# Two 256-column products in place of one of 512, and one 256-column sum, in a float32 two-block transformer kernel

## The chip, the cores and the metric

The kernel runs on one core of a Trainium2 chip. The metric is the device time of one execution in microseconds (us), the median of three runs. The page of the profile comes from one further, profiled execution.

## The reference

256 tokens of width 2048 pass through two transformer blocks, all in float32. The first has 16 heads of causal attention with forget gates and a feed-forward part with a short convolution. The second has 4 heads of gated linear attention, 8 heads of dilated attention and a gated feed-forward part. The matrices are what costs time:

```python
# block 1
q, k, v, f_logit = jnp.split(h @ w_in, [hd, 2 * hd, 3 * hd], axis=-1)      # 2048 x (3 * 2048 + 16)
...
h = h + attention(...) @ w_out                                              # 2048 x 2048
up = rms_norm(h) @ w_up                                                     # 2048 x 2 * 5632
h = h + (jax.nn.silu(gate) * val) @ w_down                                  # 5632 x 2048
# block 2
x = x + mix @ w_out[l]
h2 = rms_norm_2(x, norm2_g[l])
x = x + (jax.nn.silu(h2 @ w_gate[l]) * (h2 @ w_up[l])) @ w_down[l]
```

## The kernel before, in words

Activations stand transposed: 128 features on the partitions, 256 tokens (S) along the free axis. Every large matrix is cut into blocks of 128 x 128, and eight blocks make a unit of 512 KB. There are 784 units, and they pass through a ring of four slots. For each unit SyncE starts one transfer into `raw`; ScalarE copies it into `whi` (line 729), rounded to the format in which TensorE multiplies at its full rate; VectorE subtracts (line 1053) and gets `wlo`, what the rounding dropped. Activations are split in the same way: `xs`, `mix` and `hid2` hold for each 128 features 256 columns of the high part and, right behind, 256 of the low part (`x[:, kc, 0, :]` and `x[:, kc, 1, :]`).

A product in nearly full float32 precision is then the sum of three: high weights by high x, high weights by low x, low weights by high x. TensorE does this in `unit` (lines 370 to 382): for the eight blocks one product each of `whi` with all 512 columns of x (line 378), then for the eight blocks one product each of `wlo` with the 256 high columns (line 381), added to the right half of the bank. An output chunk of 128 features so ends as two halves of a PSUM bank of 512 float32 columns, and VectorE adds them in `fold` (line 1059), a reduction over pairs into `folded_t`. The instruction behind it reads `folded_t`: the residual sum (line 1067), the scaling by the norm (`take`, line 1093) or line 1219 for one tile of the linear attention.

The order of the work is written out by hand, one queue for each engine, tied by semaphores. `lo_ready` counts split units and lets TensorE begin a unit; `unit_used` counts finished ones and lets ScalarE refill the slot; `chunk_out` counts chunks that VectorE has taken out of a bank and lets TensorE use it again. The ring runs three units ahead (`AHEAD`). Between units TensorE has small products of the attention heads (lines 412 to 526). Four banks `acc` take the large sums, four more the small ones. The units 0 to 95 are the projections ahead of block 1's heads, then come 32 of the output projection, 176 of up, 88 of down, and the same again for block 2. The first eight blocks are in `first_half` (lines 614 to 623), where high and low products take turns as x arrives.

`chunk_folded` is a second counter: `fold` and `narrow_copy` raise it, and `narrow_sum` on TensorE (line 410) waits for it.

Of the kernel before, what the change touches and what calls it, by code (L numbers as in the profile page):

```python
# [30 lines left out]
ALU = mybir.AluOpType  # L31
ACT = mybir.ActivationFunctionType
AX_X = mybir.AxisListType.X

P = 128
S = 256
# [62 lines left out]
def build(nc, wstream, narrow_w, xt, vectors, identity, dist_onehot, rel_bias, gate_w2, scan_keep, gla_mask, fox_mask, out):  # L99
    with ExitStack() as ctx:  # L100
# [8 lines left out]
        whi = [sb(f"whi{i}", [P, UW], F32R) for i in range(RING)]  # L109
# [259 lines left out]
        def _(pe):  # L369
            def unit(pos, k, blocks, x):  # L370

                slot = pos.slot(k)
                pe.wait_ge(lo_ready, pos.unit(k) + 1)
                for j, (bank_no, kc, first, last, late) in enumerate(blocks):
                    if late:
                        pe.wait_ge(*late)
                    w_hi = whi[slot][:, j * P:(j + 1) * P]
                    pe.matmul(acc[bank_no][:, :], w_hi, x[:, kc, :, :].rearrange("p a s -> p (a s)"), start=first, stop=False)  # L378
                for j, (bank_no, kc, first, last, late) in enumerate(blocks):
                    w_lo = wlo[slot][:, j * P:(j + 1) * P]  # L380
                    mm = pe.matmul(acc[bank_no][:, S:2 * S], w_lo, x[:, kc, 0, :], start=False, stop=last)  # L381
                mm.then_inc(unit_used, 1)

            def half(pos, k, bank_no, part, x, late=None):
# [22 lines left out]
                    if kc >= KC - 4:  # L407
                        mm.then_inc(narrow_done, 1)

            def narrow_sum(chunk):  # L410
                pe.wait_ge(chunk_folded, chunk + 1)
                pe.matmul(b_turn[0:16, 0:S], quarter_sum[:, 0:16], folded_t[:, :], start=True, stop=True).then_inc(narrow_summed, 1)

            def norm_mean(n):
# [199 lines left out]
            def first_half():  # L614
                pe.wait_ge(first_lo, 1)
                for kc in range(BLOCKS):
                    if kc == BLOCKS // 2:
                        pe.wait_ge(lo_ready, 1)
                    pe.wait_ge(xs_ready, kc + 1)
                    cols = slice(kc * P, (kc + 1) * P)  # L620
                    pe.matmul(acc[1][:, :], whi[0][:, cols], xs[:, kc, :, :].rearrange("p a s -> p (a s)"), start=kc == 0, stop=False)
                    mm = pe.matmul(acc[1][:, S:2 * S], wlo[0][:, cols], xs[:, kc, 0, :], start=False, stop=False)
                mm.then_inc(unit_used, 1)

            first = Pos(L0.unit_heads)
# [43 lines left out]
            for c in range(6):  # L669
                pe.wait_ge(chunk_out, L1.chunk_in if c == 1 or c == 2 else L1.chunk_heads + c - 2)  # L670
                for part in range(2):
                    k = 2 * c + part
                    late = {}
                    if c == 0:
                        late = {8 * part: (xs_ready, 2 * KC + 8 * (part + 1) - 1), 8 * part + 7: (xs_ready, 2 * KC + 8 * (part + 1))}
                    half(Pos(L1.unit_heads), k, 1 + c % 3, part, xs, late)
                    if k == 1:
                        norm_mean(2)
                        narrow(1)
                    if k == 2:  # L680
                        narrow_sum(L1.chunk_in)
                    if k == 3:
                        gates()
                    if k == 7:
                        gla_intra(0)
                    if k == 9:
                        gla_turn_v(0, False)
                    if k == 10:
                        gla_chunk_states(0)
# [358 lines left out]
        def _(dve):  # L1048
# [3 lines left out]
                dve.wait_ge(hi_ready, pos.unit(k) + 1)  # L1052
                dve.tensor_tensor(wlo[slot][:, :], raw[slot][:, :], whi[slot][:, :], ALU.subtract).then_inc(lo_ready, 1)  # L1053

            def fold(rows, bank_no, chunk):

                if not isinstance(chunk, int) or chunk:
                    dve.wait_ge(chunk_out, chunk)
                dve.tensor_reduce(folded_t[0:rows, :], acc[bank_no][0:rows, :].rearrange("p (a s) -> p s a", a=2),  # L1059
                                  AX_X, ALU.add).then_inc(chunk_folded, 1)  # L1060
                dve.wait_ge(chunk_folded, chunk + 1)

            def add_residual(pos, k, c, chunk, bank_no):

                dve.wait_ge(unit_used, pos.unit(k))
                fold(P, bank_no, chunk)
                dve.tensor_tensor(xres[:, c, :], folded_t[:, :], xres[:, c, :], ALU.add).then_inc(chunk_out, 1)

            def norm_chunk(n, c, par, chunk_no):
                norm_lo(n, c, chunk_no)  # L1070
# [17 lines left out]
            def take(dst, bank_no, last_unit, chunk):  # L1088

                dve.wait_ge(unit_used, last_unit + 1)  # L1090
                rows = dst.shape[0]
                fold(rows, bank_no, chunk)
                dve.tensor_tensor(dst, folded_t[0:rows, :], rstd[0:rows, :], ALU.mult).then_inc(chunk_out, 1)  # L1093


            def square_low(n, which):
# [97 lines left out]
            def gla_step(g, s, pos, lag, own=True):  # L1194
# [20 lines left out]
                    return  # L1215
                if s == (2 if lag else 3):
                    dve.wait_ge(unit_used, chunk(0) + 1)
                    fold(P, 1, L1.chunk_heads + 6 * g)
                    dve.scalar_tensor_tensor(out=g_q[:, :], in0=folded_t[:, :], scalar=float(P) ** -0.5, in1=rstd[:, :],
                                             op0=ALU.mult, op1=ALU.mult).then_inc(chunk_out, 1)  # L1220
                if s == 4:
                    take(g_k[:, :], 2, chunk(1), L1.chunk_heads + 6 * g + 1)
# [425 lines left out]
```

## Time and profile before

| | |
|---|---|
| median of 3 runs | 2276.18 us (2275.83 to 2277.05) |
| profiled execution, its time | 2276.7 us |
| its span | 2274.8 us |
| PE busy | 2260.0 us (99%), 13190 products |
| weight loads (PEld) busy | 1980.8 us (87%), 13190 |
| VectorE (DVE) busy | 1623.9 us (71%) |
| ScalarE (ACT) busy | 1230.4 us (54%) |
| transfers | 421.82 MB, mean 185 GB/s |

"Busy" is the union of the records of an engine. A product's record goes from its start to the end of its passage through the array, so records of products in a row overlap, and the mean length of a record is not the distance between two. Weight loads have a row of their own, since they run beside the product in front. The chain of waits is followed back from the last instruction; its pieces don't overlap, so the length of a piece of eight products is eight times the distance between them. Its times at a start differ a little from those of the timeline, since a piece begins where the one before ended.

### The profile page before, as it was taken

The numbers are of one execution on the slowest core, as the hardware profiler recorded it, in microseconds if no ns is written. First come the engines' busy times: TensorE is split into PE (matmuls) and PEld (weight loads), VectorE is DVE, ScalarE is ACT, GpSimd is POOL, SyncE is SP. The second block draws the span as 40 slices with busy tenths as digits, with TensorE's granted clock in tenths as the row PEclk, the third lists the DMA queues.
The fourth block names the chain that finished last, engine by engine and source line by source line (L and its number), as shares of the span: only waits on it lengthen the run. The fifth ranks groups of instructions, "written<-read, shape, count | busy, mean of one in ns | idle before, by whom it ended". The sixth has DMA issues, their size and how long they took to land.

```text
span 2274.8 us, 39123 instructions
## 1 busy us (share of the span) xinstructions
PE 2260.0 (99%) x13190; PEld 1980.8 (87%) x13190; DVE 1623.9 (71%) x2378; ACT 1230.4 (54%) x1614; POOL 53.1 (2%) x78
## 2 busy tenths in 40 slices
PE   8999999999999999999999999999999999999999
PEld 6888888888888888888888888888888888888888
DVE  7877777888888888555567577777666676664554
ACT  6777765655555555444465577655444444443332
POOL 1111100000000000000000000000000000000000
PEclk9999999999999999999999999999999999999999
DMA  6555555555555555655545555555555555555654
GB/s 203 193 176 183 183 169 191 187 193 191 189 192 185 193 189 186 198 194 187 192 154 187 161 168 166 168 192 190 190 193 188 190 192 188 191 191 199 203 198 134
DMA packets 118593, 421.82 MB, mean 185 GB/s; under 512 B 13773, under 2 KB 15973, under 8 KB 118544
## 3 DMA queue, kind: packets, MB, share of 16 engines
q1 hardware_dynamic: 113760, 413.19, 55.2%
q0 software_dynamic: 2048, 5.39, 0.9%
q10 hardware_dynamic: 2736, 2.58, 0.3%
q8 instruction: 31, 0.51, 0.1%
q14 instruction: 18, 0.15, 0.0%
HBM read 418.98 MB, written 3.70 MB: 186 GB/s over the span
## 4 chain that ended last, share of the span: by engine, by line
PE 98%; DVE 1%; ACT 0%; DMA 0%; issue 0%; SPq 0%; DVEq 0%
PE acc L378 63%; PE acc L381 32%; PE b_score L435 0%; PE b_turn L440 0%; DMA xres<-xt 0%; PE b_mean L425 0%; PE b_mean L446 0%; PE b_mean L426 0%; PE b_val L432 0%; PE b_mean L447 0%; PE b_score L434 0%; PE b_mean L448 0%; ACT xs L857 0%; PE b_mean L518 0%; PE b_mean L515 0%; PE b_score L502 0%
## 5 line engine op out<-in xcount | busy, mean ns | idle before, releaser
L729 ACT ACTIVATE whi<-raw 128x1024 fp32r<-128x1024 f32 x783 | 826.3, 1059 | 826.0 <-PE acc L381 815.1
L1053 DVE TENSOR_TENSOR wlo<-raw,whi 128x1024 fp32r<-128x1024 f32 x783 | 959.9, 1229 | 376.3 <-ACT whi L729 374.3
L378 PE MATMUL acc<-xs,whi 128*128 128x512 f32 x4344 | 1094.9, 395 | 2.2 <-DVE wlo L1053 1.8
L378 PEld LDWEIGHTS acc<-xs,whi 128*128 128x128 f32 x4344 | 781.9, 188 | 146.5 <-issue 5.1
L381 PEld LDWEIGHTS acc<-xs,wlo 128*128 128x128 f32 x4344 | 583.4, 188 | 44.3
L381 PE MATMUL acc<-xs,wlo 128*128 128x256 f32 x4344 | 593.9, 279 | 0.0
L378 PE MATMUL acc<-hid,whi 128*128 128x512 f32 x1408 | 351.0, 392 | 0.0
L1059 DVE TENSOR_REDUCE folded_t<-acc 128x256 f32<-128x512 f32 x336 | 231.9, 690 | 137.9 <-PE acc L381 128.2
L378 PEld LDWEIGHTS acc<-hid,whi 128*128 128x128 f32 x1408 | 251.9, 188 | 43.2
L381 PEld LDWEIGHTS acc<-hid,wlo 128*128 128x128 f32 x1408 | 188.3, 188 | 14.4
L381 PE MATMUL acc<-hid,wlo 128*128 128x256 f32 x1408 | 191.6, 278 | 0.0
L378 PE MATMUL acc<-mix,whi 128*128 128x512 f32 x512 | 128.6, 394 | 0.0
L378 PEld LDWEIGHTS acc<-mix,whi 128*128 128x128 f32 x512 | 91.9, 188 | 16.5 <-DVE mix L1151 0.5
L381 PEld LDWEIGHTS acc<-mix,wlo 128*128 128x128 f32 x512 | 68.5, 188 | 5.2
L381 PE MATMUL acc<-mix,wlo 128*128 128x256 f32 x512 | 69.8, 279 | 0.0
L845 ACT ACTIVATE hid<-hid 128x256 f32 (+1 forms) x88 | 36.1, 410 | 53.5 <-DVE hid L1277 53.3
L1119 DVE SCALAR_TENSOR_TENSOR qk_n<-qk,qk_gain,rstd_qk 128x256 f32<-128x256 f32 x48 | 21.4, 488 | 44.2 <-ACT rstd_qk L756 44.2
L1093 DVE TENSOR_TENSOR up_g<-folded_t,rstd 128x256 f32<-128x256 f32 x88 | 37.5, 426 | 3.0
L1093 DVE TENSOR_TENSOR up_v<-folded_t,rstd 128x256 f32<-128x256 f32 x88 | 37.5, 426 | 3.0
L1281 DVE TENSOR_TENSOR hid<-hid,hid 128x256 f32 (+1 forms) x88 | 36.9, 419 | 1.0 <-ACT hid L845 1.0
L830 ACT ACTIVATE tap_g<-up_g,vec 128x256 f32<-128x256 f32 x44 | 26.5, 602 | 16.2 <-DVE up_g L1093 16.2
L838 ACT ACTIVATE tap_v<-up_v,vec 128x256 f32<-128x256 f32 x44 | 26.5, 602 | 15.1 <-DVE up_v L1093 15.0
(190 smaller groups left out, 1001.6 us busy)
## 6 DMA issues: line engine op xcount, KB each, us to landing
raw<-wstream SPq DMA_DIRECT2D x783, 512.0 KB, 4.0
decay_row<-decay_scratch POOLq DMA_DIRECT2D x16, 128.0 KB, 3.7
out<-xres ACTq DMA_DIRECT2D x16, 128.0 KB, 2.4
xres<-xt SPq DMA_DIRECT2D x3, 512.0 KB, 8.4
dist_scratch<-bias_scratch POOLq DMA_DIRECT2D x8, 192.0 KB, 4.6
toeplitz<-dist_scratch POOLq DMA_DIRECT2D x8, 128.0 KB, 3.9
xres<-xt SPq DMA_DIRECT2D x2, 256.0 KB, 4.6
raw<-wstream SPq DMA_DIRECT2D x2, 256.0 KB, 5.6
```

The lines of the kernel that those rows point to most:

```text
L378: pe.matmul(acc[bank_no][:, :], w_hi, x[:, kc, :, :].rearrange("p a s -> p (a s)"), start=first, stop=False)
L381: mm = pe.matmul(acc[bank_no][:, S:2 * S], w_lo, x[:, kc, 0, :], start=False, stop=last)
L729: act.activation(whi[slot][:, :], raw[slot][:, :], ACT.Copy).then_inc(hi_ready, 1)
L830: act.activation(tap_g[:, :], up_g[:, 0:S], ACT.Identity, scale=column("conv0", j), bias=column("convb", j)).then_inc(tap0, 1)
L838: act.activation(tap_v[:, :], up_v[:, 0:S], ACT.Identity, scale=column("conv0", FC + j), bias=column("convb", FC + j)).then_inc(tap0, 1)
L845: act.activation(hid2[:, j, 0, :], hid[:, :], ACT.Copy).then_inc(hid_hi_ready, 1)
L1053: dve.tensor_tensor(wlo[slot][:, :], raw[slot][:, :], whi[slot][:, :], ALU.subtract).then_inc(lo_ready, 1)
L1059: dve.tensor_reduce(folded_t[0:rows, :], acc[bank_no][0:rows, :].rearrange("p (a s) -> p s a", a=2), AX_X, ALU.add).then_inc(chunk_folded, 1)
L1093: dve.tensor_tensor(dst, folded_t[0:rows, :], rstd[0:rows, :], ALU.mult).then_inc(chunk_out, 1)
L1119: dve.scalar_tensor_tensor(out=qk_n[:, a, :], in0=qk[:, a, :], scalar=qk_gain[:, col + a:col + a + 1], in1=rstd_qk[:, a, :], op0=ALU.mult, ...
L1281: dve.tensor_tensor(hid2[:, j, 1, :], hid[:, :], hid2[:, j, 0, :], ALU.subtract).then_inc(hid_split, 1)
```

## The change

In `unit` the product with 512 columns becomes two runs: eight products of `whi` with the 256 high columns, then eight of `whi` with the 256 low columns, then, as before, eight of `wlo` with the high columns. All three add to columns 0 to 255 of the bank. `first_half` does the same for each of its blocks, without the runs. `fold` is gone: VectorE's instruction that used to read `folded_t` reads the bank. `chunk_folded` is raised by `narrow_copy` alone, so `narrow_sum` waits for 1 and 2.

```diff
--- before.py
+++ after.py
@@ -375,10 +375,13 @@
                     if late:
                         pe.wait_ge(*late)
                     w_hi = whi[slot][:, j * P:(j + 1) * P]
-                    pe.matmul(acc[bank_no][:, :], w_hi, x[:, kc, :, :].rearrange("p a s -> p (a s)"), start=first, stop=False)
+                    pe.matmul(acc[bank_no][:, 0:S], w_hi, x[:, kc, 0, :], start=first, stop=False)
+                for j, (bank_no, kc, first, last, late) in enumerate(blocks):
+                    w_hi = whi[slot][:, j * P:(j + 1) * P]
+                    pe.matmul(acc[bank_no][:, 0:S], w_hi, x[:, kc, 1, :], start=False, stop=False)
                 for j, (bank_no, kc, first, last, late) in enumerate(blocks):
                     w_lo = wlo[slot][:, j * P:(j + 1) * P]
-                    mm = pe.matmul(acc[bank_no][:, S:2 * S], w_lo, x[:, kc, 0, :], start=False, stop=last)
+                    mm = pe.matmul(acc[bank_no][:, 0:S], w_lo, x[:, kc, 0, :], start=False, stop=last)
                 mm.then_inc(unit_used, 1)
 
             def half(pos, k, bank_no, part, x, late=None):
@@ -407,8 +410,8 @@
                     if kc >= KC - 4:
                         mm.then_inc(narrow_done, 1)
 
-            def narrow_sum(chunk):
-                pe.wait_ge(chunk_folded, chunk + 1)
+            def narrow_sum(n):
+                pe.wait_ge(chunk_folded, n + 1)
                 pe.matmul(b_turn[0:16, 0:S], quarter_sum[:, 0:16], folded_t[:, :], start=True, stop=True).then_inc(narrow_summed, 1)
 
             def norm_mean(n):
@@ -618,8 +621,9 @@
                         pe.wait_ge(lo_ready, 1)
                     pe.wait_ge(xs_ready, kc + 1)
                     cols = slice(kc * P, (kc + 1) * P)
-                    pe.matmul(acc[1][:, :], whi[0][:, cols], xs[:, kc, :, :].rearrange("p a s -> p (a s)"), start=kc == 0, stop=False)
-                    mm = pe.matmul(acc[1][:, S:2 * S], wlo[0][:, cols], xs[:, kc, 0, :], start=False, stop=False)
+                    pe.matmul(acc[1][:, 0:S], whi[0][:, cols], xs[:, kc, 0, :], start=kc == 0, stop=False)
+                    pe.matmul(acc[1][:, 0:S], whi[0][:, cols], xs[:, kc, 1, :], start=False, stop=False)
+                    mm = pe.matmul(acc[1][:, 0:S], wlo[0][:, cols], xs[:, kc, 0, :], start=False, stop=False)
                 mm.then_inc(unit_used, 1)
 
             first = Pos(L0.unit_heads)
@@ -678,7 +682,7 @@
                         norm_mean(2)
                         narrow(1)
                     if k == 2:
-                        narrow_sum(L1.chunk_in)
+                        narrow_sum(1)
                     if k == 3:
                         gates()
                     if k == 7:
@@ -1052,19 +1056,10 @@
                 dve.wait_ge(hi_ready, pos.unit(k) + 1)
                 dve.tensor_tensor(wlo[slot][:, :], raw[slot][:, :], whi[slot][:, :], ALU.subtract).then_inc(lo_ready, 1)
 
-            def fold(rows, bank_no, chunk):
-
-                if not isinstance(chunk, int) or chunk:
-                    dve.wait_ge(chunk_out, chunk)
-                dve.tensor_reduce(folded_t[0:rows, :], acc[bank_no][0:rows, :].rearrange("p (a s) -> p s a", a=2),
-                                  AX_X, ALU.add).then_inc(chunk_folded, 1)
-                dve.wait_ge(chunk_folded, chunk + 1)
-
             def add_residual(pos, k, c, chunk, bank_no):
 
                 dve.wait_ge(unit_used, pos.unit(k))
-                fold(P, bank_no, chunk)
-                dve.tensor_tensor(xres[:, c, :], folded_t[:, :], xres[:, c, :], ALU.add).then_inc(chunk_out, 1)
+                dve.tensor_tensor(xres[:, c, :], acc[bank_no][:, 0:S], xres[:, c, :], ALU.add).then_inc(chunk_out, 1)
 
             def norm_chunk(n, c, par, chunk_no):
                 norm_lo(n, c, chunk_no)
@@ -1089,8 +1084,7 @@
 
                 dve.wait_ge(unit_used, last_unit + 1)
                 rows = dst.shape[0]
-                fold(rows, bank_no, chunk)
-                dve.tensor_tensor(dst, folded_t[0:rows, :], rstd[0:rows, :], ALU.mult).then_inc(chunk_out, 1)
+                dve.tensor_tensor(dst, acc[bank_no][0:rows, 0:S], rstd[0:rows, :], ALU.mult).then_inc(chunk_out, 1)
 
 
             def square_low(n, which):
@@ -1215,8 +1209,7 @@
                     return
                 if s == (2 if lag else 3):
                     dve.wait_ge(unit_used, chunk(0) + 1)
-                    fold(P, 1, L1.chunk_heads + 6 * g)
-                    dve.scalar_tensor_tensor(out=g_q[:, :], in0=folded_t[:, :], scalar=float(P) ** -0.5, in1=rstd[:, :],
+                    dve.scalar_tensor_tensor(out=g_q[:, :], in0=acc[1][:, 0:S], scalar=float(P) ** -0.5, in1=rstd[:, :],
                                              op0=ALU.mult, op1=ALU.mult).then_inc(chunk_out, 1)
                 if s == 4:
                     take(g_k[:, :], 2, chunk(1), L1.chunk_heads + 6 * g + 1)
```

TensorE's queue in the loop over the attention heads of block 1, in the kernel before (`xs` is the split x; x8 are eight products in a row; REGISTER_ALU and ISA rows are waits and registers):

```order
L373 ISA
L378 MATMUL acc<-xs,whi 128x512 x8
L381 MATMUL acc<-xs,wlo 128x256 x8
L373 REGISTER_ALU
L378 MATMUL acc<-xs,whi 128x512 x8
L381 MATMUL acc<-xs,wlo 128x256 x8
L444 REGISTER_ALU
L446 MATMUL b_mean<-probs_t,v_tok 128x128
L447 MATMUL b_mean<-probs_t,v_tok 128x128
L448 MATMUL b_mean<-probs_t,v_tok 128x128
```

and in the changed kernel (lines 449 to 451 are the former 446 to 448):

```order
L373 REGISTER_ALU
L378 MATMUL acc<-xs,whi 128x256 x8
L381 MATMUL acc<-xs,whi 128x256 x8
L384 MATMUL acc<-xs,wlo 128x256 x8
L373 REGISTER_ALU
L378 MATMUL acc<-xs,whi 128x256 x8
L381 MATMUL acc<-xs,whi 128x256 x8
L384 MATMUL acc<-xs,wlo 128x256 x8
L449 MATMUL b_mean<-probs_t,v_tok 128x128
L450 MATMUL b_mean<-probs_t,v_tok 128x128
L451 MATMUL b_mean<-probs_t,v_tok 128x128
```

Each unit has three runs of eight where it had two, and the small products between units stand where they stood.

VectorE's queue in the up projection, from the end of the first turn to the loop, in the kernel before (`up_g` and `up_v` are chunks of the gate and value sides):

```order
L1053 TENSOR_TENSOR wlo<-raw,whi 128x1024
L1059 TENSOR_REDUCE folded_t<-acc 128x256
L1093 TENSOR_TENSOR up_g<-folded_t,rstd 128x256
L1053 TENSOR_TENSOR wlo<-raw,whi 128x1024
L1449 UNCONDITIONAL_BRANCH
L1449 ISA
L1058 ISA
L1059 TENSOR_REDUCE folded_t<-acc 128x256
L1061 REGISTER_ALU
L1093 TENSOR_TENSOR up_v<-folded_t,rstd 128x256
L1257 REGISTER_ALU
L1258 ISA
L1258 SCALAR_TENSOR_TENSOR tap_g<-up_g,vec,tap_g 128x256
```

and in the changed kernel:

```order
L1057 TENSOR_TENSOR wlo<-raw,whi 128x1024
L1087 TENSOR_TENSOR up_g<-acc,rstd 128x256
L1057 TENSOR_TENSOR wlo<-raw,whi 128x1024
L1442 UNCONDITIONAL_BRANCH
L1442 ISA
L1087 TENSOR_TENSOR up_v<-acc,rstd 128x256
L1250 ISA
L1251 ISA
L1251 SCALAR_TENSOR_TENSOR tap_g<-up_g,vec,tap_g 128x256
```

The reduction ahead of each chunk's instruction is gone, and that instruction reads `acc`; the splits of units keep their places.

## Rows read from the trace of the kernel before

**Rows 1.** The page: busy time by engine; the span in 40 slices (busy tenths, PEclk)

```profile
PE 2260.0 (99%) x13190; PEld 1980.8 (87%) x13190; DVE 1623.9 (71%) x2378; ACT 1230.4 (54%) x1614; POOL 53.1 (2%) x78
...
PEclk9999999999999999999999999999999999999999
```

**Rows 2.** The chain that ended last, whole span, shares by line

```profile
by line: PE acc L378 62.8%; PE acc L381 31.8%; PE b_score L435 0.5%; PE b_turn L440 0.3%; DMA xres<-xt 0.3%; PE b_mean L425 0.3%; PE b_mean L446 0.3%; PE b_mean L426 0.2%; PE b_val L432 0.2%; PE b_mean L447 0.2%; PE b_score L434 0.2%; PE b_
```

**Rows 3.** Waits of PE, the four longest: engine line waited for, total us, times, longest us

```profile
PE acc L621 <- DVE wlo L1299: 7.3, 1, 7.3
PE acc L378 <- DVE wlo L1053: 1.8, 1, 1.8
PE acc L621 <- DVE xs L1076: 0.9, 1, 0.9
PE b_mean L425 <- DVE sq_lo L1098: 0.6, 1, 0.6
```

**Rows 4.** Groups by line: engine op, tiles, shapes, count | busy us, mean ns | idle before

```profile
L1053 DVE TENSOR_TENSOR wlo<-raw,whi 128x1024 fp32r<-128x1024 f32 x783 | 959.9, 1229 | 376.3 <-ACT whi L729 374.3
L378 PE MATMUL acc<-xs,whi 128*128 128x512 f32 x4344 | 1094.9, 395 | 2.2 <-DVE wlo L1053 1.8
...
L381 PE MATMUL acc<-xs,wlo 128*128 128x256 f32 x4344 | 593.9, 279 | 0.0
...
L1059 DVE TENSOR_REDUCE folded_t<-acc 128x256 f32<-128x512 f32 x336 | 231.9, 690 | 137.9 <-PE acc L381 128.2
```

**Rows 5.** Groups by line of DVE, two operations of 256 columns

```profile
L1067 DVE TENSOR_TENSOR xres<-folded_t,xres 128x256 f32<-128x256 f32 (+1 forms) x64 | 27.2, 425 | 5.2 <-DVE folded_t L1059 3.0
...
L1130 DVE TENSOR_TENSOR biased<-b_score,decay_row 128x256 f32<-128x256 f32 x16 | 6.6, 414 | 0.0
```

**Rows 6.** The chain in the down projection, 1000 to 1014 us: start us, us, what

```profile
1001.04 0.91 PE acc L381 x8
1001.95 1.83 PE acc L378 x8
1003.77 0.94 PE acc L381 x8
```

**Rows 7.** The chain in the up projection, 600 to 606 us

```profile
601.30 0.94 PE acc L381 x8
602.25 1.83 PE acc L378 x8
604.08 0.91 PE acc L381 x8
```

**Rows 8.** The chain with heads, 102.29 to 119.72 us, six whole units

```profile
by line: PE acc L378 63.2%; PE acc L381 32.3%; PE b_turn L440 1.9%; PE b_mean L425 1.3%; PE b_mean L426 1.3%
...
112.76 0.94 PE acc L381 x8
...
116.00 0.94 PE acc L381 x8
...
118.78 0.94 PE acc L381 x8
```

**Rows 9.** The chain at the end, 2262 to 2275 us

```profile
2267.74 0.91 PE acc L381 x8
2268.65 1.83 PE acc L378 x8
2270.47 0.95 PE acc L381 x8
...
2271.45 0.70 DVE folded_t L1059
...
2272.18 0.42 DVE xres L1067
```

**Rows 10.** Timeline, 1000 to 1010 us: start us, us, engine line op

```profile
1000.65 1.10 PEld L381 LDWEIGHTS acc<-hid,wlo 128*128 128x128 f32 x8
```

## The prediction

> **What bounds the kernel.** I read the page's first part first. TensorE (PE) is busy for 2260.0 of 2274.8 us, VectorE for 71% of it [rows 1]. Matmul records last longer than the distance between two starts, so "busy" alone proves little; the chain of waits does. It gives 62.8% of the span to the 512-column products of line 378 and 31.8% to the 256-column products of line 381, and everything that isn't TensorE together is about 2% [rows 2]. The list of waits then says whether TensorE ever stands still for another engine: the four longest entries make 10.6 us, 8.2 of them at the very first half unit (lines 1299 and 1076) and 1.8 at one other unit; all others are below 0.5 us [rows 3]. So the time is the number of columns that TensorE streams, times what a column costs there, plus a start and a tail. VectorE's own queue (783 splits of a unit at 1229 ns, 336 folds at 690 ns [rows 4]) lies beside that.
>
> One thing in those numbers matters for the rest: records of a 512-column product last 395 ns and of a 256-column one 279 ns [rows 4]. These are latencies of overlapping instructions. What counts is a run of eight: in the steady part the chain shows 1.83 us for eight products of 512 columns and 0.91 or 0.94 us, in turn, for eight of 256 [rows 6].
>
> **The change, part by part.** Per unit of eight blocks the eight 512-column products (x high and x low side by side) become two runs of eight 256-column products with the same weights, and the third run is as before. There are 783 units outside the first one and 6264 blocks in them; columns streamed stay 768 for a block, products (and with each a weight load) go from 12,528 to 18,792.
>
> *First term, TensorE.* Nothing in the arithmetic is saved, so the question is what two 256-column products cost against one of 512. The trace has both, on the same tiles, with the granted clock at the top level (2.4 GHz, a 9 in every slice of [rows 1]), so no foreign price is needed.
> By shares [rows 2]: two products of 256 columns are 2 x 31.8 = 63.6% of the span, the 512-column ones that they replace 62.8%; 0.8% of 2274.8 us is +18.2 us. Each share is rounded, which leaves +-3.4 us.
> By pieces: in the steady part a run of eight costs 0.925 us on average (0.91 and 0.94), two of them 1.85, against 1.83: +0.02 us for a unit [rows 6]. It is the same in the up projection, where VectorE folds after every second unit [rows 7]. In the part with heads six whole units fill 17.43 us, of which 63.2% (11.02 us) are the wide runs and 32.3% (5.63 us) the narrow ones: 2 x 5.63 - 11.02 = 0.24 us, or +0.04 for a unit [rows 8]. With some 190 units in the projections ahead of the heads of both blocks and 593 others that is 190 x 0.04 + 593 x 0.02 = 7.6 + 11.9 = +19.5 us. Between 18.2 and 19.5 I take +19 us, which is 3 ns for a block.
> The additional 6264 weight loads are inside this: in the runs of 256 columns each product has its own load of 128 columns, and the loads of a run of eight span 1.10 us, just as the products do [rows 10]; they overlap the stream there and will in the new run.
>
> The Trainium skill weighs against the change here: "TensorE: Matmul & The Clock Gate", section "Back-to-back issue gap", gives N/2.4 + 2.5 ns between warm products. By it a split of 512 into twice 256 adds one fixed 2.5 ns, an estimate of 6264 x 2.5 = +15.7 us. The trace disagrees with the level (229 ns against 215.8, and 116 against 109.2) and comes close on the difference (2 x 115.6 - 228.8 = 2.4 ns in the steady part). The same section gives a sustained roofline of 131 ns at N=512, which the 229 ns of [rows 6] contradict; I make nothing of it.
>
> *Second term, the two levels.* The unknown is not the average but which level the new runs take. The narrow runs take 0.91 and 0.94 us in turn, unit by unit, and the level alternates whatever runs beside them: the last three units, for which the kernel has no weight left to load or split beside them (`AHEAD` is 3), show the same 0.91, 1.83, 0.95 [rows 9]. The wide runs between them carry the engine from one level to the other. With no wide run left the alternation may go on, or the engine may stay on one level. Bounds: all runs at 0.91 make a unit 2.73 us, against 2.755 now in the 593 and 2.775 in the 190 units ((5.63 + 11.02)/6): -0.025 x 593 - 0.045 x 190 = -23.4 us. All at 0.94 make 2.82: +0.065 x 593 + 0.045 x 190 = +47.1 us, and +59 if the true value is 0.945 (0.95 appears too). The pieces are rounded to 0.01 us, which on three runs of 783 units is some +-12 us. I take the mean of the levels, since both are about as frequent in the trace; both ends stay in the range.
>
> *Third term, VectorE.* 336 folds of 690 ns go, 231.9 us of its time [rows 4]; the instruction behind each now reads PSUM itself. A 256-column operation of two tensors takes 425 ns where both are in SBUF (line 1067) and 414 where one is in PSUM (line 1130) [rows 5], so the instructions that stay keep their length within 11 ns each, 4 us in all, and some 232 us go. Worth on the path: nothing, except at the end, since TensorE waits for VectorE only at the start, and there for the splits of the first weights, which stay. After the last product the chain is fold 0.70, residual 0.42, then the store [rows 9]: the fold goes, -0.7 us, and at most 0.01 changes beside it. The accumulator banks are freed earlier, but no wait of TensorE on them is in [rows 3], so nothing follows.
>
> *Fourth, the start.* The first eight blocks are paced by x and by the first split [rows 3]: 8.2 us of waiting in which a third instruction for each block hides. Zero, at most 8 x 3 ns either way.
> The sum narrow_sum only waits for another count of the same copy: zero.
>
> Sum: the profiled execution takes 2276.7 us, a span of 2274.8 and 1.9 around it. +19 - 0.7 = +18.3 gives a span of 2293.1 and a time of 2295.0. That execution is 0.5 us above the median of 2276.2, so the forecast for the median is **2294.5 us**.
>
> **Rivals.**
> A. *One level, the slow one* (0.94 throughout): 2276.2 + 47 to 59 - 0.7, so 2322 to 2335, middle 2328. For it: with small products between units (lines 440, 425 and 426) the runs stay at 0.94 three units in a row [rows 8], so a disturbance seems to lead to the slow level, and without wide runs there is nothing known that leaves it. Against it: the fast level returns within two or three units today.
> B. *One level, the fast one* (0.91 throughout): the place is every run of every unit, the price -23.4 - 0.7 (with rounding -12 to -36), time 2252. It decides for faster as soon as three runs together stay under 2.755 us, 0.918 each. For it: long unbroken runs of equal instructions are what a steady rhythm would need, and 0.91 is in the trace for half of the steady units. Against: 0.94 is at least as frequent.
> C. *VectorE's relief speeds TensorE*, since a fold reads PSUM and the splits read SBUF while products stream. The most that it could pay is the whole distance between the levels and the average. But the pieces are equal to 0.01 us where VectorE is busy (up projection, [rows 7]), where it is much less so (down projection, [rows 6]) and with nothing beside (the end, [rows 9]). I count it for nothing.
> D. *A column costs what a column costs*, and the split is free: 2276.2 - 0.7 = 2275.5, no change.
> That the change doesn't do what it says can be left out: the order of instructions shows three runs of eight with 256 columns.
>
> **How the numbers follow.** No change means within 0.2% (4.6 us), about what a measurement of this kernel can tell. The mixed forecast, 2284 to 2304: 0.42. Rival A: 0.28. Rival B: 0.20. Rival D with what lies near it: 0.10, of which 0.08 within the bound and the rest slower. So faster 0.20, same 0.08, slower 0.72. The range from 2251 to 2331 takes in A and about half of B; the forecast's own range is 2284 to 2304. If B and A were equally likely they would roughly cancel, but the predicted time is that of the likeliest case.
>
> **What would show it.** In the chain of the changed kernel three lines, 378, 381 and 384, should each have close to 31.6% of a span some 18 us longer (0.925 us x 783 = 724 us of 2293). Steady pieces of 0.91 and 0.94 in turn say mixed; one value only says A or B. The list of waits of TensorE should stay near 11 us; VectorE should fall from 1624 to about 1392 us busy. The end of the chain should hold one VectorE instruction, not two. Wrong would be: pieces of the 256-column runs outside 0.90 to 0.95 us, a new wait of TensorE for VectorE or ScalarE, or line 381 (x low) costing other than line 384 (same width, other weights).

## The result and the profile after

The changed kernel takes 2333.41 us (median of 4 runs, 2331.47 to 2337.94) against 2276.01 us (4 runs) before: a ratio of 1.0253, 95% interval 1.024 to 1.0266. It is 57.4 us slower. The forecast of 2294.5 us got the sign and missed the size, and the range ended at 2331. Rival A, which had 2322 to 2335 us, is what happened, with a cost beside it that nobody had forecast.

Engines and the code-fetch queue on the page of the changed kernel (profiled execution 2337.94 us, the longest of the four, span 2336.2):

```profile
PE 2315.1 (99%) x19462; PEld 2293.8 (98%) x19462; DVE 1410.7 (60%) x2042; ACT 1205.5 (52%) x1614; POOL 53.0 (2%) x78
...
q8 instruction: 66, 1.08, 0.2%
```

VectorE is busy for 213 us less. The 336 folds took 231.9 us by their own records [rows 4]; part of that overlapped the records beside them, which "busy" counts once. The instructions that now read PSUM kept their length (`up_g` 424 ns on average, 426 before). The weight loads are now busy for 98% of the span (87% in [rows 1]). The shares of the chain:

```profile
by line: PE acc L378 31.6%; PE acc L381 31.5%; PE acc L384 31.5%; PE b_score L438 0.4%; PE b_turn L443 0.3%; DMA xres<-xt 0.3%; ACT whi L733 0.3%; PE b_mean L428 0.2%; PE b_mean L429 0.2%; PE b_val L435 0.2%; PE b_score L437 0.2%; PE b_mean
```

Three runs of 31.5 or 31.6% make 94.6% of 2336.2 us = 2210 us, where [rows 2] had 94.6% of 2274.8 = 2152. So 58 of the 61 us that the span grew by lie in the large products. The steady part, start us, us, what, which answers to [rows 6]:

```profile
1020.52 0.94 PE acc L381 x8
1021.46 0.94 PE acc L384 x8
1022.40 0.94 PE acc L378 x8
```

Every narrow run takes 0.94 us here. The 0.91 of [rows 6] is gone in all units without heads. With heads of block 1 it is the same, on both sides of the small products of lines 428 and 429, where [rows 8] already showed mostly 0.94:

```profile
111.89 0.94 PE acc L384 x8
112.83 0.24 PE b_mean L428
113.06 0.23 PE b_mean L429
113.30 0.94 PE acc L378 x8
```

Only among the heads are there exceptions, about 6% of the units there, such as this one behind small products of block 2 (start us, us, what):

```profile
1208.85 0.44 PE b_val L493 x4
1209.29 0.91 PE acc L378 x8
1210.20 0.91 PE acc L381 x8
```

The end answers to [rows 9]; the fold is gone there, as forecast:

```profile
2332.56 0.96 PE acc L384 x8
...
2333.54 0.42 DVE xres L1062
```

The waits of TensorE (engine line waited for: total us, times, longest us) answer to [rows 3]:

```profile
PE acc L624 <- DVE wlo L1292: 7.4, 1, 7.4
PE acc L378 <- issue: 4.3, 1, 4.3
PE acc L378 <- DVE wlo L1057: 3.3, 2, 2.8
PE acc L378 <- DVE mix L1145: 1.2, 2, 0.6
PE acc L381 <- issue: 1.2, 1, 1.2
```

Beside the known 7.4 us at the start there are new ones. "issue" means that the profile shows nothing that line 378 waited for. The two "issue" waits lie in the down projection of block 1, where the loop of two passes jumps back; the 2.8 us that are put down to line 1057 lie at the same jump in block 2. The busy time by engine in block 1 (PE, PEld, DVE, ACT, POOL), then the granted clock (PEclk), the share of the DMA engines and GB/s:

```profile
1030.00:1040.00 10.00, 10.00 (x87) 10.00 (x86) 4.88 (x6) 3.73 (x4) 0.00 (x0) 1.00 0.55 173
1040.00:1046.00 6.00, 2.19 (x19) 1.98 (x17) 3.61 (x5) 2.28 (x4) 0.00 (x0) 1.00 0.62 188
1046.50:1049.50 3.00, 2.44 (x10) 2.14 (x10) 0.00 (x0) 0.00 (x0) 0.00 (x0) 0.50 0.30 116
1049.50:1060.00 10.50, 9.91 (x71) 9.91 (x72) 2.45 (x2) 2.91 (x3) 0.00 (x0) 0.82 0.18 55
```

TensorE stands for 4.3 us, from 1042.2 us on, runs at 0.50 of its clock (1.2 GHz) in the third stretch and is back at the upper level only within the fourth.

### The profile page after: what moved, and what is told of

Read it like the earlier page. It is cut to its first block, busy times and chain, and to the rows that moved or that the text cites. A ratio compares the mean times of both kernels' runs of the same rounds, so it can differ in the third digit from the quotient of the medians.

```text
span 2336.2 us, 50800 instructions
## 1 busy us (share of the span) xinstructions
PE 2315.1 (99%) x19462; PEld 2293.8 (98%) x19462; DVE 1410.7 (60%) x2042; ACT 1205.5 (52%) x1614; POOL 53.0 (2%) x78
## 4 chain that ended last, share of the span: by engine, by line
PE 98%; ACT 1%; DVE 0%; DMA 0%; issue 0%; SPq 0%; ACTq 0%; DVEq 0%
PE acc L378 32%; PE acc L381 32%; PE acc L384 32%; PE b_score L438 0%; PE b_turn L443 0%; DMA xres<-xt 0%; ACT whi L733 0%; PE b_mean L428 0%; PE b_mean L429 0%; PE b_val L435 0%; PE b_score L437 0%; PE b_mean L449 0%; PE b_mean L450 0%; PE b_mean L451 0%; ACT xs L861 0%
## 5 line engine op out<-in xcount | busy, mean ns | idle before, releaser
L378 PE MATMUL acc<-xs,whi 128*128 128x256 f32 x4344 | 609.7, 282 | 0.9 <-DVE wlo L1057 0.6
L381 PE MATMUL acc<-xs,whi 128*128 128x256 f32 x4344 | 599.5, 280 | 0.0
L378 PEld LDWEIGHTS acc<-xs,whi 128*128 128x128 f32 x4344 | 553.7, 188 | 10.4 <-issue 5.1
L381 PEld LDWEIGHTS acc<-xs,whi 128*128 128x128 f32 x4344 | 549.9, 188 | 0.0
L384 PEld LDWEIGHTS acc<-xs,wlo 128*128 128x128 f32 x4344 | 549.2, 188 | 0.0
L378 PE MATMUL acc<-hid,whi 128*128 128x256 f32 x1408 | 196.2, 281 | 7.1 <-issue 4.3
L381 PE MATMUL acc<-hid,whi 128*128 128x256 f32 x1408 | 195.8, 281 | 1.2 <-issue 1.2
L378 PEld LDWEIGHTS acc<-hid,whi 128*128 128x128 f32 x1408 | 179.8, 189 | 7.4 <-issue 4.5
L381 PEld LDWEIGHTS acc<-hid,whi 128*128 128x128 f32 x1408 | 179.6, 189 | 1.4 <-issue 1.4
L384 PEld LDWEIGHTS acc<-hid,wlo 128*128 128x128 f32 x1408 | 178.9, 188 | 0.0
L378 PE MATMUL acc<-mix,whi 128*128 128x256 f32 x512 | 72.0, 281 | 1.2 <-DVE mix L1145 1.2
L381 PE MATMUL acc<-mix,whi 128*128 128x256 f32 x512 | 70.6, 279 | 0.0
L378 PEld LDWEIGHTS acc<-mix,whi 128*128 128x128 f32 x512 | 65.2, 188 | 1.9 <-DVE mix L1145 1.6
L1087 DVE TENSOR_TENSOR up_g<-acc,rstd 128x256 f32<-128x256 f32 x88 | 37.4, 424 | 48.2 <-PE acc L384 43.6
L381 PEld LDWEIGHTS acc<-mix,whi 128*128 128x128 f32 x512 | 64.8, 188 | 0.0
L1087 DVE TENSOR_TENSOR up_v<-acc,rstd 128x256 f32<-128x256 f32 x88 | 37.3, 424 | 43.6 <-PE acc L384 43.6
```

The source lines that it names most:

```text
L378: pe.matmul(acc[bank_no][:, 0:S], w_hi, x[:, kc, 0, :], start=first, stop=False)
L381: pe.matmul(acc[bank_no][:, 0:S], w_hi, x[:, kc, 1, :], start=False, stop=False)
L384: mm = pe.matmul(acc[bank_no][:, 0:S], w_lo, x[:, kc, 0, :], start=False, stop=last)
L1087: dve.tensor_tensor(dst, acc[bank_no][0:rows, 0:S], rstd[0:rows, :], ALU.mult).then_inc(chunk_out, 1)
```

## The experiments

All times are medians of a kernel's runs beside runs of the kernel before on the same chip.

**e1_split_only: one half of the change alone.** In the kernel before only this is changed:

```diff
-    pe.matmul(acc[bank_no][:, :], w_hi, x[:, kc, :, :].rearrange(...), start=first, stop=False)
+    pe.matmul(acc[bank_no][:, 0:S], w_hi, x[:, kc, 0, :], start=first, stop=False)
+for j, (bank_no, kc, first, last, late) in enumerate(blocks):
+    w_hi = whi[slot][:, j * P:(j + 1) * P]
+    pe.matmul(acc[bank_no][:, S:2 * S], w_hi, x[:, kc, 1, :], start=False, stop=False)
```

> The kernel before with line 378's 512-column product split into two runs of eight of 256 columns, and nothing else: the halves of the bank and the folds on VectorE stay. Theory (narrow runs alone stay on the slow level, 117.7 ns a product): all three runs 0.94 us, 2331 to 2336 us, as the changed kernel. Rival 1 (three passes over the same 256 columns of the bank bring the slow level): the runs go to 0.91 or alternate, 2250 to 2300 us. Rival 2 (the missing folds on VectorE shift the rhythm of the engines): alternation comes back, about 2295 us.

Measured: 2334.53 us, ratio 1.0249 (1.0232 to 1.0266). The chain in the down projection:

```profile
1021.00 0.94 PE acc L381 x8
1021.94 0.94 PE acc L384 x8
```

This is the changed kernel's time, with all folds in place (VectorE 1624.6 us busy). So the one sum and the missing folds cost and bring nothing that can be measured (their own runs spread by 6.5 us in the changed kernel and 4.6 in this one); the split does all of it. Both rivals fall.

**e2_down_twice: the loop's jump.**

```diff
-with pe.Fori(0, 2) as i:
-    pos = Pos(layer.unit_down, U_DOWN // 2, i)
+for i in range(2):
+    pos = Pos(layer.unit_down + i * U_DOWN // 2)
```

> The changed kernel with TensorE's down projection written out twice instead of a loop of two passes over 44 units. Theory (the body with 50% more instructions no longer stays in the instruction buffer, so the jump back waits for code, and the clock falls to 1.2 GHz behind it): the gaps of 4.5 us at 1042 us and 3.0 us at 2205 us and the stretches at the lower clock behind them go, 2333.4 - 8 to 14 = 2319 to 2325 us. Rival (the gap belongs to the weights' transfer or to VectorE's split there, and code is not short): gaps stay, 2331 to 2335 us.

Measured: 2324.89 us (2324.55 to 2325.37), 8.5 us less than the changed kernel's median, ratio 1.0213 (1.0196 to 1.023). The spans of the two profiled executions differ by 13.3 us, since that of the changed kernel was its longest. Two of the four stretches shown above:

```profile
1040.00:1046.00 6.00, 6.00 (x54) 6.00 (x53) 3.91 (x6) 2.84 (x5) 0.00 (x0) 1.00 0.62 186
1046.50:1049.50 3.00, 3.00 (x28) 3.00 (x27) 1.40 (x2) 1.06 (x1) 0.00 (x0) 1.00 0.58 206
```

TensorE is busy throughout and the clock stays at 1.00. That the jump back costs this time is shown. The code fetches (q8, packets of 16 KB) say why it does so now. In the changed kernel, during the second pass in block 1 (1042 to 1148 us), the queue shows

```profile
q8 instruction: 9, 0.15, 0.5%
```

and the first three of them start at 1044, 1048 and 1051 us, in the stall and in the slow stretch behind it; the later ones lie some 14 us apart. In the kernel before, q8 has 6 packets in the first pass (905 to 1020 us) and none in the second (1020 to 1148 us). So the longer body is fetched again for its second pass and the shorter one was not. Written out twice it is fetched as well (7 packets from 1045 to 1148 us), but TensorE never stands: what costs is not the fetching but, as it seems, that at a jump it comes too late. (The totals, 31 packets before, 66 after and 61 in e2_down_twice, also hold the code that simply got longer.) How much code stays in place was not measured.

**e3_stream_columns: less to stream, the same to load.** The third run is cut to w columns, one w for each stage:

```diff
-mm = pe.matmul(acc[bank_no][:, 0:S], w_lo, x[:, kc, 0, :], start=False, stop=last)
+mm = pe.matmul(acc[bank_no][:, 0:w], w_lo, x[:, kc, 0, 0:w], start=False, stop=last)
```

> The changed kernel with the third run (low weights by high x) cut to fewer columns by stage: 256 in the heads part of block 1, 192 in its output projection, 128 in up, 224 in down, then 160, 64, 240, 96 in block 2; the product of the low weights is left out for the other columns. Loads stay at 128 columns each. Theory load (the weight load sets the distance between narrow products): the third run stays at 0.94 us for eight at all widths from 240 down to 64. Theory stream (columns set it, 0.44 ns each and some ns fixed): 0.71 us for eight at 192 columns, 0.48 at 128, 0.25 at 64.

Measured: 2299.77 us (one run). In the output projection of block 2, where the third run (line 390) streams only 64 columns, the chain and, below it, the weight loads of that run on the timeline:

```profile
1502.99 0.94 PE acc L387 x8
1503.93 0.81 PE acc L390 x8
1504.75 1.02 PE acc L384 x8
```

```profile
1503.66 0.98 PEld L390 LDWEIGHTS acc<-mix,wlo 128*128 128x128 f32 x8
```

The pieces are 0.94, 0.81 and 1.02: 2.77 us for a unit, where full width takes 2.83. The third run ends sooner by the columns that its last product lacks, and the first run behind it waits for its load by as much; with 128 columns (up projection of block 1) and 240 (that of block 2) the sum is 2.77 too. So a quarter of the columns saves next to nothing. Eight loads take 0.98 us up to the end of the last record; less the 0.19 us of that record, seven distances of 112 ns. The products of this run start as far apart, so with so few columns the loads set the distance. The theory "stream" (0.25 us at 64 columns) is refuted. The theory "load" is not borne out as it stands either, since 112 ns is less than the 117.7 of the full run. And with 192 columns (output projection of block 1) a unit takes 2.72 us, because there the second run, of which nothing was changed, takes 0.91:

```profile
351.40 0.94 PE acc L384 x8
352.34 0.91 PE acc L387 x8
353.24 0.87 PE acc L390 x8
```

**e4_load_columns: less to load, the same to stream.** The second run loads m columns of weights, one m for each stage:

```diff
-    w_hi = whi[slot][:, j * P:(j + 1) * P]
-    pe.matmul(acc[bank_no][:, 0:S], w_hi, x[:, kc, 1, :], start=False, stop=False)
+    w_hi = whi[slot][:, j * P:j * P + m]
+    pe.matmul(acc[bank_no][0:m, 0:S], w_hi, x[:, kc, 1, :], start=False, stop=False)
```

> The changed kernel with the second run (high weights by low x) loading fewer weights by stage: 128 columns of weights in the heads part of block 1, 96 in its output projection, 64 in up, 32 in down, then 128, 64, 96, 32 in block 2; that product is left out for the other output features. Each product still streams 256 columns. Theory load (the weight load sets the distance): the second run falls from 0.94 us to where the stream alone sets it, about 0.87 us (256 columns at 2.4 GHz, 107 ns each, and little more). Theory stream (the load is hidden): 0.94 us for eight stays in every stage.

Measured: 2302.91 us (one run). The first pieces are from the output projection of block 1 (m = 96), with the change of level in them:

```profile
343.92 0.94 PE acc L387 x8
344.85 0.91 PE acc L390 x8
345.76 0.91 PE acc L384 x8
346.67 0.91 PE acc L387 x8
```

and these from the up projection of block 1 (m = 64):

```profile
600.95 0.94 PE acc L387 x8
601.88 0.94 PE acc L390 x8
```

Neither theory fits. A shorter load did not bring the second run (line 387) to 0.87 us, so its own 256 columns hold it at 0.91 at least. But with m = 96 all three runs went to 0.91 and stayed there, those with full loads too; with m = 64 they stayed at 0.94, give or take 0.01. With m = 32 the down projection of block 1 was slow and that of block 2, behind a stage at 0.91, was fast. In the slow one even 32-column loads left the second run at 0.93 us, 116.5 ns a product, so the load isn't what makes the slow level slow. Load (112 ns in e3_stream_columns) and a whole step (113.3 ns at best) are so close for 256 columns that shortening the load gains almost nothing. The run has two levels, and the engine mostly keeps the one it has.

**e5_kick96 and e6_kick64: can the level be set?** In four units of each block, between the first and the second run (down written out twice as in e2):

```diff
+if not pos.per and kicked(pos.base + k):
+    for j, (bank_no, kc, first, last, late) in enumerate(blocks):
+        pe.matmul(b_val[0:96, 0:S], whi[slot][:, j * P:j * P + 96], x[:, kc, 0, :], start=True, stop=True)
```

> The changed kernel with the down projection written out twice (2324.9 us by itself) and, in four units of each block (the fifth of the output projection, the third of up, the first and seventh of down), eight additional products between the first and the second run: 96 columns of the high weights by high x into a bank that nobody reads then. They compute nothing that is used. Theory (two levels of a run of 256-column products, 113.3 and 117.7 ns a product; a level stays until something disturbs it, and a run that loads 96 columns of weights leads to the fast one): some 570 units go from 2827 to 2720 ns, -61 us, the eight runs cost 8 x 8 x 0.113 = 7 us: 2268 to 2278 us. Rival (the fast level of the kernel with shorter loads came from the product left out, in every unit): 2324.9 + 7 = 2332 us.

> The same as e5_kick96 with 64 columns of weights in the additional products instead of 96. Theory (the length of the disturbance decides, and 64 leads to the slow level as in the stages that loaded 64): 2324.9 + 7 = 2332 us. Rival (any additional run of products leads to the fast level): as e5_kick96, 2268 to 2278 us.

Measured: 2276.27 us for 96 (10 runs, 2269.97 to 2277.24; ratio 0.9994, 0.9985 to 1.0004) and 2332.24 us for 64 (2 runs). The chain of e5_kick96 at the start of the up projection:

```profile
422.43 0.91 PE acc L393 x8
423.34 0.43 PE b_mean L432 x2
423.77 0.94 PE acc L384 x8
424.71 0.91 PE b_val L387 x8
425.62 0.91 PE acc L390 x8
426.52 0.91 PE acc L393 x8
```

The small products of line 432 (a mean) throw the engine from 0.91 to 0.94, and the eight additional products (`b_val`) bring it back; it then stays for the rest of the stage. With 64 columns it doesn't:

```profile
600.78 0.94 PE acc L390 x8
601.73 0.94 PE acc L393 x8
```

So 56 us, the distance between e5_kick96 and e6_kick64, hang on how many weights are loaded in eight runs that compute nothing. The level is a state. The heads of both blocks, which have no additional runs, stay mostly slow in both. The executions of e5_kick96 fall into groups, three near 2270 and six near 2277 us with one between; the profiled one is of the first, and what the others lack was not seen.

**e7_mixed_widths: narrow where it stays fast, wide elsewhere.**

```diff
+wide = (pos.base + k) % U_LAYER < U_IN
...
+if wide:
+    pe.matmul(acc[bank_no][:, :], w_hi, x[:, kc, :, :].rearrange("p a s -> p (a s)"), start=first, stop=False)
+    continue
```

with `fold` put back for those chunks.

> e5_kick96, but the projections ahead of the heads keep the 512-column products, the halves of the bank and VectorE's folds of the kernel before (190 units). Theory: those units go back from some 2827 ns to 2780 ns, 190 x 0.047 = -9 us against e5_kick96: 2259 to 2269 us, faster than both kernels. Rival (the levels in the later stages are inherited and differ with another stage in front): up and down fall back to 0.94 us a run, 2315 to 2325 us.

Measured: 2263.32 us (4 runs, 2263.19 to 2269.53), ratio 0.9952 (0.9935 to 0.9968), as the theory had it: the later stages keep 0.91 us a run with another stage in front. The down projection is written out twice and the additional runs of e5_kick96 are in it, so this isn't the split alone.

**e8_x_at_64, e12_x_at_0 and e9_before_x_at_64: where x lies.** The split activations `xs`, `mix` and `hid2` start 192 bytes into a 256-byte line. The constant sets that start by a gap in front of `xs`, so all tiles behind it in SBUF shift with it; `raw`, `whi`, `wlo` and `xres` lie in front and stay. Moved, in the changed kernel (64 and 0) and in the kernel before (64):

```diff
-X_AT = 192
+X_AT = 64
```

> The changed kernel with the split x placed 64 bytes into a 256-byte line instead of 192. Theory (the level is a matter of timing, not of addresses): 0.94 us a run stays, 2330 to 2338 us. Rival (the reads of x and of the weights collide by address): the runs take another length and the time moves by more than 10 us.

> The changed kernel with x at the start of a 256-byte line. Theory (the place decides the level): a third place takes one of the two levels throughout the later stages, either 2260 to 2268 us (fast) or 2330 to 2338 us (slow); a level between them, or both mixed, would say that more than two states exist. Rival (192 was special, as the only slow place): fast.

> The kernel before with x placed 64 bytes into a 256-byte line instead of 192 and nothing else. Theory (the place of x decides which level a narrow run falls into after a disturbance, and the wide runs of this kernel disturb every unit): the narrow runs stop alternating and take 0.91 us each, 783 x 0.015 to 0.03 us = 12 to 24 us less, 2252 to 2264 us. Rival (the place matters only to unbroken narrow runs): 0.91 and 0.94 go on in turn, 2274 to 2278 us.

Measured: 2263.57 us for the changed kernel at 64 (one run), 2356.99 us at 0 (2 runs, ratio 1.0353, 1.0332 to 1.0374), and 2287.98 us for the kernel before at 64 (4 runs, ratio 1.0049, 1.0032 to 1.0066). None of the three theories held: for e8_x_at_64 the rival came true, for e9_before_x_at_64 the narrow runs stopped alternating as forecast but the time rose, and e12_x_at_0 came out slower than either level allows. The chain in the up projection, first of the changed kernel at 64:

```profile
601.24 0.91 PE acc L384 x8
602.15 0.91 PE acc L378 x8
```

at 0:

```profile
601.09 0.95 PE acc L378 x8
602.04 0.95 PE acc L381 x8
```

and of the kernel before at 64:

```profile
601.77 1.86 PE acc L378 x8
603.63 0.91 PE acc L381 x8
```

At 64 the narrow runs outside the heads take 0.91 with no additional run anywhere (among the heads about 6 in 10 do): 70 us by one constant. The single execution is borne out by the four of e10_x_at_64_twice below. At 0 there are further lengths, mostly 0.95, which I had excluded. In the kernel before the narrow run does stop alternating (0.91 each time), but the wide one goes from the 1.83 of [rows 7] to 1.86, and the kernel loses 11 us against the 2276.85 beside it. In this kernel 192 suits wide products, 64 narrow ones. Whether x alone does this, or one of the tiles that shift with it, was not separated; in the units of the up projection TensorE reads only `whi`, `wlo` and `xs`.

**e11_x_at_64_kick64: state or place?** The lines of e6_kick64 in e10 below.

> e10_x_at_64_twice with the runs of additional 64-column loads of e6_kick64. Theory (the place decides where a disturbance leads): 0.91 us a run comes back behind each additional run, 2255 + 7 = 2262 us. Rival (the level is a state alone, and the place only happened to start it well): the 64-column runs lead to the slow level, which stays, 2310 to 2322 us.

Measured: 2261.14 us (2 runs, 2259.34 and 2262.93). The up projection, behind a run of 64-column loads:

```profile
601.45 0.91 PE acc L384 x8
```

At 192 (e6_kick64) the same stage is slow behind that run to its end, at 64 it is fast. The additional run isn't what makes it fast: here the eight products of `b_val` already take 0.91 us, and in e10_x_at_64_twice, without any, the engine is back at 113 ns within one run behind the small products. So outside the heads the engine comes back by itself at 64, and at 192 it stays slow; the state alone doesn't explain it.

**e10_x_at_64_twice: both costs taken away.** X_AT = 64 and the down projection written out twice.

> The changed kernel with x at 64 bytes and TensorE's down projection written out twice. Theory (both costs are separate): 2263.6 - 8.5 = 2255 us, faster than every kernel so far, 0.990 to 0.993 of the kernel before. Rival (the fast level of e8_x_at_64 was luck of one execution, as e5_kick96 shows two groups of times): a spread of over 10 us between executions and a median above 2265 us.

Measured: 2252.35 us (2252.1 to 2252.62), ratio 0.9894 (0.9877 to 0.991): 81 us less than the changed kernel and 24.5 less than the kernel before (2276.85 beside it), and the fastest kernel of the study. Against e8_x_at_64 the jump is worth 11 us here, against 8.5 forecast. The chain's shares of its span of 2250.3 us:

```profile
by line: PE acc L378 31.9%; PE acc L384 31.7%; PE acc L381 31.7%; PE b_score L438 0.5%; PE b_turn L443 0.3%; DMA xres<-xt 0.3%; PE b_mean L429 0.3%; PE b_val L435 0.2%; PE b_mean L428 0.2%; PE b_score L437 0.2%; PE b_mean L449 0.2%; PE b_me
```

## Why the prediction was wrong, by its steps

*What bounds the kernel*: right. Only TensorE's queue moved the time. VectorE's 336 folds brought nothing that can be measured, as e1_split_only shows from the other side.

*First and second term, +19 us*: the arithmetic on the average was right, its use was not. It assumed that narrow runs would keep the mix of 0.91 and 0.94 us that they had between wide ones. The step that failed stands in the second term: "I take the mean of the levels, since both are about as frequent in the trace". They were that frequent because, with x at this place, the engine changed level between wide runs, which the same paragraph says. Without them it stays (e1_split_only): 0.94 throughout is +47.1 - 0.7 = +46.4 us by the working of that term, and e2_down_twice, the change without the jump's cost, measured 2324.89 us, 48.4 above the 2276.45 beside it. Of the 57 us measured some 48 are this level, where the forecast had 18, and the rest is the jump. The bound was good and the choice inside it was bad. [rows 8] held a hint towards the slow end: behind small products 0.94 came three times in a row, although wide runs stood between. It could not decide, for with x at 64 the same small products leave most runs fast. And the stated range left out the top of its own rival A: A was priced up to 2335, the range ended at 2331.

*The weight loads*: "they overlap the stream there and will in the new run" was right, but took hidden for harmless. e3_stream_columns shows that loads of 128 columns alone need 112 ns a product, where a step of the narrow run takes 113.3 or 117.7: the load is hidden with 2 to 6 ns to spare. Behind a wide product, 229 ns, it has more than 100. [rows 10] couldn't tell: a load's record lasts 188 ns, longer than the distance between two starts, so the records of a narrow run overlap whether the load has slack or not. That the load causes the slow level is not shown; e4_load_columns, where a quarter of it left 116.5 ns, speaks against it.

*Not in the prediction at all*: the jump back in the down projection, 8.5 us, of which the trace of before had no wait. Without it the time would have been inside the range, which would not have made the mean of the levels any better. The forecast list of what to look for ("a new wait of TensorE") did catch it.

*Third and fourth term*: -0.7 us at the end and nothing at the start, as seen. VectorE fell to 1410.7 us and not to about 1392, since the prediction took the folds' own records for busy time; nothing hung on it.

*Rival A* had the right mechanism, and its 2322 to 2335 us hold with the jump (2333.41) and without it (2324.89). *Rival B* (fast throughout, 2252 us) was no fancy: with x at 64 and the jump gone, e10_x_at_64_twice takes 2252.35 us. That the figure fits to a microsecond is luck, for among the heads some 4 in 10 narrow runs are still slow there. The change is good in another layout. *Rival C* (VectorE's relief) is refuted by e1_split_only. The fixed 2.5 ns for a product, which the Trainium skill gives in "TensorE: Matmul & The Clock Gate", section "Back-to-back issue gap", is not what a split costs here: at the slow level it costs 2 x 117.7 - 229 = 6 ns, at the fast one it gives 229 - 2 x 113.3 = 2 ns back. The 2.4 ns of the prediction, so close to it, were the mean of the two levels.

What stays open: why a 256-column product has these lengths (113.3, 117.7 and about 119 ns between starts, 120 in some stages at 0), and what in a disturbance decides the level. That the load alone takes nearly as long as the whole step is shown; that its reads and those of x meet in the memory is only a guess from the dependence on the place.

## What to carry to other kernels

When a wide product is split, count the weight loads as well as the columns: if load and stream are of about the same length, the hidden one has hardly any slack left. In this kernel small things (a disturbance, the place of an operand) then set the pace; that the one follows from the other was not shown. After such a change tune the layout again, since a constant that is the better one for the old shape can be the worse one for the new. And when a trace shows two speeds of the same instruction in turn, find what switches them before averaging; if the change removes the switch, forecast the ends, not the middle.

## What the runs showed of the hardware that I had not expected

- A run of eight 256-column products in this format takes 0.91 or 0.94 us (113.3 or 117.7 ns each) and keeps its level over hundreds of units; with x at 192 a mean on another bank switches it to the slow one and eight products with 96-column loads to the fast one (e5_kick96), while 64-column loads don't (e6_kick64).
- The start of the moving operand in a 256-byte line (with the tiles behind it) moves the whole kernel by 93 us: 2263.57 us at 64, 2333.41 at 192, 2356.99 at 0. For 512-column products the order of 64 and 192 is the other way round (2287.98 and 2276.85 us).
- A product of 64 columns behind a load of 128 costs as much as one of 240 (e3_stream_columns, a unit of 2.77 us in both stages); the products then start 112 ns apart, as the loads do.
- A jump back over a longer loop body, with the code fetched again behind it, stopped TensorE for 4.3 us in one block and 2.8 in the other, and the granted clock was 0.50 behind it: 8.5 us between the medians for the two loops.
